# Summing two expert results onto the scaled row with identity matmuls instead of on VectorE and ScalarE

## The chip, the cores and the metric

The kernel runs on 1 core of one Trainium2 chip. The metric is the device time of one execution in microseconds (us). A lower number is better.

## The reference, cut to what matters

A first block ends in a mixture of experts. Each token takes the best two of the 8 experts of its best group, so every token has exactly two results, each with its own weight. The experts' sum is added to ALPHA times the row (ALPHA is the fourth root of 2), a layer norm follows, and the second block opens with an RMS norm of that row.

```python
def _moe(x, wr_g, br_g, wr_e, br_e, w_gate, w_up, w_down):
    ...
        lv, esel = lax.top_k(le, MOE_TOPK)
        we = jax.nn.softmax(lv, axis=-1) * ptop
        ...
        h = jax.nn.silu(hg) * hu * gate[..., None].astype(xs.dtype)
        return jnp.einsum('seh,ehd->sd', h, w_down)

def _layer_norm(x, g, b):
    mu = jnp.mean(xf, -1, keepdims=True)
    var = jnp.mean(jnp.square(xf - mu), -1, keepdims=True)
    return ((xf - mu) * lax.rsqrt(var + LN_EPS) * g + b).astype(x.dtype)

def _rms_norm(x, g, eps=1e-6):
    return (xf * lax.rsqrt(jnp.mean(xf * xf, -1, keepdims=True) + eps) * g).astype(x.dtype)
```

There are 512 tokens of 1024 values, 32 experts with 256 hidden units, and all data is float32.

## The kernel before, in words

The program is a row of **stages** (`Core.stage`, L152). Each stage is one block with a program per engine, and a barrier over all engines closes it, so nothing of a stage starts before the slowest engine of the stage before has come to its end. Inside a stage the engines meet by semaphores only. Three stages matter here.

**choose** (L745 to L870) picks the experts from the router's logits. VectorE carries a long chain; TensorE counts and then builds, for each expert, the list of at most CAP = 64 tokens (L785, one-hot `where` times `whom`). ScalarE takes three exponentials. GpSimd issues two gathers of rows (L804). At the end VectorE writes the two weights of each token into `pair` (L868, L869), token by token.

**experts_by_token** (L989 to L1192) runs the 32 experts one after the other. SyncE (SP) fetches 3 MB of weights for each, into three slots. ScalarE and VectorE split gate and up weights into a rounded part and its rest (L1135, L1176), TensorE multiplies (L1087, L1088), sums (L1096), and forms the results, `down` (L1108). `y_rows` (L1137 to L1143) copies the results of an expert from PSUM by two ScalarE copies of 64x512, and GpSimd scatters them by an indirect DMA (L1054) to `y_dram`, a DRAM buffer with the first results of all tokens in rows 0 to 511 and the second ones in rows 512 to 1023. After the last scatter GpSimd waits until all scatters have landed (L1066, L1067), and then the stage can end. A second way through the program (`results_to_pairs`, L1195), taken when an expert has more than 64 tokens, isn't run with these inputs.

**pairs_end** (L1217 to L1332) takes four tiles of 128 tokens through the following steps, tile by tile:
- SP loads first and second results (L1240, 512 KB each) and, between them, the three rows of gains, each broadcast to 128 partitions (L1242, 512 KB each); then three weight slabs of 1 MB for the next stage (L1244). Two loads of 2 KB that belong to the next stage (`sinks`, L174) stand ahead of all of these.
- ScalarE scales the first result by its weight (`weigh`, L1266). VectorE adds the second result times its weight (L1302) and then ALPHA times the row (L1303).
- ScalarE takes the negative mean (L1275), the sum of squares around it (L1277) and the root (L1278).
- VectorE centres and multiplies by the gain (L1310), inverts the root (L1312), scales and adds the bias (L1315). SP stores that row (L1247).
- ScalarE squares it again and takes a root (L1284, L1285), VectorE inverts (L1326) and makes `h` (L1331), TensorE transposes `h` in eight 128x128 pieces (L1256), ScalarE copies them out rounded (`x_hi`, L1290, two halves) and VectorE takes the rest (`x_lo`, L1321, two halves).

The order on each engine is written out by hand: in round s, VectorE does the sum of tile s, the two row steps of tile s-1, `x_lo` of tile s-2, and `h` of tile s-1. The next stage opens with a weight split (L1477, L1507) and the first matmuls on the rows just made (L1556).

Of the kernel before, what the change touches and what calls it, by code (L numbers as in the profile page):

```python
# [15 lines left out]
F32 = mybir.dt.float32  # L16
# [6 lines left out]
P = 128  # L23
# [721 lines left out]
def choose(c, lg, pair_gates, e, taken, table, most, x_dram, first):  # L745
# [5 lines left out]
    with ExitStack() as ctx:  # L751
# [5 lines left out]
        place, whom = c.sb(ctx, "place", [P, 2, NT]), c.sb(ctx, "whom", [P, 2, NT, 2, NE])  # L757
        where, most_u = c.sb(ctx, "where", [P, 2, NT, CAP]), c.sb(ctx, "most_u", [P, 1], mybir.dt.uint32)
        ps = c.ps(ctx, "lists", [P, 2, 512])
        to_exp, exps, chain, picked, counted, listed, placed, most_ready, cleared, stored = (  # L760
            c.sem(x) for x in ("to_exp", "exps", "dve", "picked", "counted", "listed", "placed", "most_ready", "cleared", "stored"))
        counts = ps[:, 0, 0:(NT + 1) * NE].rearrange("p (i e) -> p i e", e=NE)
        ahead, total = counts[:, 0:NT, :], counts[:, NT, :]
        lists = ps[0:CAP, 1, 0:2 * NE].rearrange("p (w e) -> p w e", w=2)
        xg, gi, xg_in, indexed = first
        with c.stage() as block:
# [7 lines left out]
            def _(pe):  # L774
# [34 lines left out]
            def _(dve):  # L809
# [58 lines left out]
                run(nc.vector.tensor_copy(pair_gates[:, :, 0:1], st[:, :, 4:5]))  # L868
                run(nc.vector.tensor_tensor(pair_gates[:, :, 1:2], st[:, :, 1:2], st[:, :, 4:5], ALU.mult))  # L869
# [119 lines left out]
def experts_by_token(c, table, x_dram, y_dram, w_gate, w_up, w_down, room_yg, small, wgu, wd, gu_in, d_in, first):  # L989
# [8 lines left out]
    with ExitStack() as ctx:  # L998
# [11 lines left out]
        scattered = [c.pool_dma_sem("scattered") for _ in range(2)]  # L1010
# [7 lines left out]
        with c.stage() as block:  # L1018
# [13 lines left out]
            def _(pool):  # L1032
# [33 lines left out]
                for u in range(2):  # L1066
                    pool.wait_ge(scattered[u], 16 * NE // 2)  # L1067
# [55 lines left out]
            def _(act):  # L1123
# [13 lines left out]
                def y_rows(j):  # L1137
# [57 lines left out]
def results_to_pairs(c, y, y_dram, pair):  # L1195

    nc = c.nc
    with ExitStack() as ctx:
        none = c.sb(ctx, "none", [P, D])
        filled, stored = c.sem("filled"), c.sem("stored")  # L1200
        with c.stage() as block:
            @block.sync
            def _(sp):
                sp.wait_ge(filled, 3)
# [3 lines left out]
                sp.wait_ge(stored, 16 * (NT + 1))  # L1208

            @block.vector  # L1210
            def _(dve):
                nc.vector.memset(none[:], 0.0).then_inc(filled, 1)
                nc.vector.memset(pair[:, :, 0:1], 1.0).then_inc(filled, 1)
                nc.vector.memset(pair[:, :, 1:2], 0.0).then_inc(filled, 1)


def pairs_end(c, y_dram, pair, room, rows_to, gain, bias, pre, x_hi, x_lo, opening):  # L1217
# [3 lines left out]
    with ExitStack() as ctx:  # L1221
        r, gb, h = c.sb(ctx, "pairs", [P, 2, NT, D]), c.sb(ctx, "gains", [P, 3, D]), c.sb(ctx, "h", [P, 2, D])
        sq, st, eps = c.sb(ctx, "sq", [P, D]), c.sb(ctx, "stat", [P, NT, 8]), c.sb(ctx, "eps", [P, 2])
        ps = c.ps(ctx, "turned", [P, 8, 512])
        rows_out = c.sem("rows_out")
        gains_in = [c.sem("gains_in") for _ in range(3)]
        pair_in = [c.sem("pair_in") for _ in range(NT)]
        eps_ready, weighed, summed, meaned, rooted, rowed, pre_rooted, h_ready, turned, x_rounded, x_split, chain, act_chain = (
            c.sem(x) for x in ("eps", "weighed", "summed", "meaned", "rooted", "rowed", "pre_rooted", "h", "turned", "x_rounded",
                               "x_split", "dve", "act"))  # L1230

# [3 lines left out]
        with c.stage() as block:  # L1235
            @block.sync
            def _(sp):
                for i in range(NT):
# [2202 lines left out]
```

## Time and profile before

| | |
|---|---|
| median of 3 runs | 2440.09 us (2439.96 to 2444.48) |
| the profiled execution's own time | 2443.96 us |
| its span, first to last instruction | 2442.1 us |
| mean granted TensorE clock | 0.931 of full speed |
| busy share: TensorE, VectorE, ScalarE, GpSimd | 90%, 56%, 37%, 5% |
| choose | from 771.4 to 793.5 us of the span |
| experts_by_token | from 793.5 to about 1104.9 us |
| pairs_end | from about 1110.4 to 1165.0 us |

In the rows, PE is TensorE's matmul, PEld its weight load, DVE is VectorE, ACT ScalarE, POOL GpSimd and SP SyncE. An engine's name with a q (SPq, POOLq) is its instruction queue. PEclk is the clock that TensorE was granted: 1.00 is 2.4 GHz and 0.50 is 1.2 GHz. A number in square brackets is idle time of the engine before the instruction, with what ended it.

### The profile page before, as it was taken

What the parts mean: (1) busy time and instruction counts of PE and PEld (TensorE: products, weight loads), DVE (VectorE), ACT (ScalarE), POOL (GpSimd) and SP (SyncE); (2) the same over time, 40 slices, a digit from 0 to 9 for tenths busy, and PEclk for the clock granted to TensorE, in tenths of its full rate; (3) what the DMA queues carried; (4) which work ended last, traced back from release to release, by engine and by line L of the source; (5) the groups of instructions that cost most, each with busy time, mean ns of one, the idle gap of its engine ahead of it and who ended that gap; (6) DMA issues with size and microseconds to landing.
All of it is one profiled execution on the core that took longest, in us unless ns stands there. A gap on an engine that the chain in (4) does not pass through costs nothing. (4 is left out here: it accounts for less than half of the span.)

```text
span 2442.1 us, 30103 instructions
## 1 busy us (share of the span) xinstructions
PE 2202.9 (90%) x11232; PEld 1664.2 (68%) x11232; DVE 1360.9 (56%) x2391; ACT 906.1 (37%) x1538; POOL 122.2 (5%) x153
## 2 busy tenths in 40 slices
PE   6798998899996999991899989999979998899997
PEld 4587765556776666650777768888757766788886
DVE  2652446856445655544345585964444456778544
ACT  3521233123232666654333433332333334233323
POOL 0000002200000232320000000000000000000000
PEclk8885999999997999995999989999989999999999
DMA  5220431231423899975332113322423222141313
GB/s 162 88 74 1 125 93 54 62 100 44 124 91 143 317 366 358 369 269 184 99 100 66 65 61 104 99 87 87 143 78 103 79 62 65 57 143 64 108 48 112
DMA packets 218989, 296.45 MB, mean 121 GB/s; under 512 B 48861, under 2 KB 183085, under 8 KB 210617
## 3 DMA queue, kind: packets, MB, share of 16 engines
q1 hardware_dynamic: 213722, 286.09, 35.0%
q0 software_dynamic: 5120, 8.40, 1.1%
q8 instruction: 92, 1.51, 0.3%
q14 instruction: 55, 0.45, 0.1%
HBM read 283.12 MB, written 22.07 MB: 125 GB/s over the span
## 5 line engine op out<-in xcount | busy, mean ns | idle before, releaser
L1556 PE MATMUL acc<-x_hi,w_hi 128*128 128x512 f32 x1432 | 579.3, 405 | 19.5 <-DVE w_lo L1507 16.2
L1557 PE MATMUL acc<-x_lo,w_hi 128*128 128x512 f32 x1432 | 566.0, 395 | 0.0
L1558 PE MATMUL acc<-x_hi,w_lo 128*128 128x512 f32 x1432 | 565.2, 395 | 0.0
L1477 ACT CAST w_hi<-raw 128x1024 fp32r<-128x1024 f32 x179 | 186.9, 1045 | 621.5 <-PE acc L1558 587.0
L1507 DVE TENSOR_TENSOR w_lo<-raw,w_hi 128x1024 fp32r<-128x1024 f32 x174 | 212.7, 1224 | 292.6 <-ACT w_hi L1477 289.3
L1556 PEld LDWEIGHTS acc<-x_hi,w_hi 128*128 128x128 f32 x1432 | 273.8, 191 | 84.2 <-DVE w_lo L1507 17.2
L1558 PEld LDWEIGHTS acc<-x_hi,w_lo 128*128 128x128 f32 x1432 | 273.2, 191 | 60.3
L1557 PEld LDWEIGHTS acc<-x_lo,w_hi 128*128 128x128 f32 x1432 | 274.0, 191 | 57.9 <-issue 2.0
L1176 DVE TENSOR_TENSOR w_lo<-wgu,w_hi 128x1024 fp32r<-128x1024 f32 x128 | 151.0, 1220 | 61.3 <-ACT w_hi L1135 60.7
L1135 ACT CAST w_hi<-wgu 128x1024 fp32r<-128x1024 f32 x128 | 127.9, 1047 | 38.6 <-DMA wgu<-in_moe_w_up 33.2
L1108 PE MATMUL ps<-wd,y 128*64 128x512 f32 x256 | 116.7, 598 | 0.7 <-DVE y L1192 0.7
L1087 PE MATMUL ps<-w_hi,xs 128*128 128x512 f32 x256 | 104.2, 407 | 3.3 <-DVE w_lo L1176 3.0
L1088 PE MATMUL ps<-w_lo,xs 128*128 128x512 f32 x256 | 101.4, 396 | 0.0
L1694 ACT ACTIVATE probs<-scores,stat 128x256 f32<-128x256 f32 (+3 forms) x96 | 51.8, 540 | 126.1 <-DVE stat L1656 125.9
L1516 DVE SCALAR_TENSOR_TENSOR sg<-sg,br 128x512 f32<-128x512 f32 x112 | 76.3, 682 | 35.4 <-PE br L1745 28.2
L2291 DVE SCALAR_TENSOR_TENSOR y_t<-pad,w,y_t 128x512 f32<-128x512 f32 x120 | 90.1, 751 | 3.4
L1703 ACT COPY probs_t<-t_ps 128x256 f32<-128x256 f32 (+3 forms) x96 | 39.0, 406 | 130.5 <-PE t_ps L1617 130.5
L1743 PE MATMUL br<-y_hi,b_hi 128*128 128x512 f32 x176 | 70.9, 403 | 15.6 <-DVE b_lo L1735 15.3
L1488 ACT ACTIVATE sg<-acc 128x512 f32<-128x512 f32 x112 | 66.2, 591 | 30.3 <-PE acc L1558 30.2
L1556 PE MATMUL acc<-x_hi,lead_hi 128*128 128x512 f32 x184 | 76.0, 413 | 1.3 <-PEq L157 1.0
L1557 PE MATMUL acc<-x_lo,lead_hi 128*128 128x512 f32 x184 | 73.5, 399 | 0.0
L1558 PE MATMUL acc<-x_hi,lead_lo 128*128 128x512 f32 x184 | 73.4, 399 | 0.0
(554 smaller groups left out, 3357.7 us busy)
## 6 DMA issues: line engine op xcount, KB each, us to landing
raw<-in_w_in SPq DMA_DIRECT2D x60, 1024.0 KB, 5.5
raw<-in_w_gate SPq DMA_DIRECT2D x40, 1024.0 KB, 5.5
wgu<-in_moe_w_gate SPq DMA_DIRECT2D x32, 1024.0 KB
wgu<-in_moe_w_up SPq DMA_DIRECT2D x32, 1024.0 KB
wd<-in_moe_w_down SPq DMA_DIRECT2D x32, 1024.0 KB, 5.3
raw_b<-in_w_branch SPq DMA_DIRECT2D x56, 256.0 KB, 2.8
room<-in_w_out SPq DMA_DIRECT2D x3, 2048.0 KB, 8.4
y_t<-in_w_out SPq DMA_DIRECT2D x3, 2048.0 KB, 10.8
```

The source lines that it names most:

```text
L1087: pe.matmul(ps[:, 0, :], xs[:, u, k, :], w_hi[:, k, :], start=(k == 0), stop=False)
L1088: mm = pe.matmul(ps[:, 0, :], xs[:, u, k, :], w_lo[:, k, :], start=False, stop=(k == KT - 1))
L1108: mm = pe.matmul(ps[0:CAP, 1 + 2 * u + half, :], ht[:, u, m * CAP:(m + 1) * CAP], wd[:, j % SLOTS, m, half * 512:half * 512 + 512], start= ...
L1135: nc.scalar.copy(part(w_hi, p), raw_part(j, p)).then_inc(w_rounded, 1)
L1176: nc.vector.tensor_tensor(part(w_lo, p), raw_part(j, p), part(w_hi, p).bitcast(F32), ALU.subtract).then_inc(w_split, 1)
L1477: self.nc.scalar.copy(self.w_hi[n % 2], self.weights(n)).then_inc(self.rounded, 1)
L1507: eng.tensor_tensor(self.w_lo[n % 2], self.weights(n), self.w_hi[n % 2].bitcast(F32), ALU.subtract).then_inc(self.split, 1)
L1516: self.nc.vector.scalar_tensor_tensor(sg, sg, 1.0, self.br[:], ALU.add, ALU.mult).then_inc(self.mixed, 1)
L1556: pe.matmul(acc, hi, tile.hi[:, k, :], start=(k == 0), stop=False)
L1557: pe.matmul(acc, hi, tile.lo[:, k, :], start=False, stop=False)
L1558: mm = pe.matmul(acc, lo, tile.hi[:, k, :], start=False, stop=(k == KT - 1))
L2291: run(nc.vector.scalar_tensor_tensor(conf[:, m, :], src, wt, conf[:, m, :], ALU.mult, ALU.add))
```

## The change

- **choose** makes no weights by token. It spreads each token's two weights over the experts (`share`, two VectorE multiplications of 128x128) and collects them by expert and place in the list with eight more matmuls (`where` times `share`, 32 columns each) and one ScalarE copy of 64x32 into `weights`.
- **y_rows** multiplies each result row by its weight as it is copied out: the two copies become two activations of the kind Copy with a scale for each partition.
- **experts_by_token** no longer waits for the scatters at its end; SP waits for them in pairs_end, ahead of its loads of results.
- **pairs_end** has TensorE sum: ALPHA times the identity times the row (2 matmuls of 128x128 by 128x512 float32 for each tile), and the identity times the first and the second result (2 matmuls each), all into the same two PSUM banks. `weigh`, L1302 and L1303 go. ScalarE and VectorE read the sum from PSUM. VectorE now does the row steps of tile s in round s, then `h` of tile s-1, then `x_lo` of tile s-2.
- The first row of gains is loaded ahead of all others, the small `sinks` loads come last.

```diff
@@ choose @@
+                pe.wait_ge(shared, 2)
+                for r in range(2):
+                    for i in range(NT):
+                        mm = pe.matmul(of_lists, where[:, r, i, :], share[:, r, i, :], start=(r == 0 and i == 0), stop=(r == 1 and i == NT - 1))
+                mm.then_inc(weighed, 1)
...
+                act.wait_ge(weighed, 1)
+                nc.scalar.copy(weights, of_lists)
...
-                run(nc.vector.tensor_copy(pair_gates[:, :, 0:1], st[:, :, 4:5]))
-                run(nc.vector.tensor_tensor(pair_gates[:, :, 1:2], st[:, :, 1:2], st[:, :, 4:5], ALU.mult))
+                run(nc.vector.tensor_tensor(st[:, :, 5:6], st[:, :, 1:2], st[:, :, 4:5], ALU.mult))
+                for r in range(2):
+                    nc.vector.tensor_tensor(share[:, r], sel[:, r], st[:, :, 4 + r:5 + r].broadcast_to([P, NT, NE]), ALU.mult
+                                            ).then_inc(shared, 1)
@@ experts_by_token @@
-                for u in range(2):
-                    pool.wait_ge(scattered[u], 16 * NE // 2)
...
-                        nc.scalar.copy(yg[:, u, half * 512:half * 512 + 512], ps[0:CAP, 1 + 2 * u + half, :]).then_inc(y_out, 1)
+                        nc.scalar.activation(yg[:, u, half * 512:half * 512 + 512], ps[0:CAP, 1 + 2 * u + half, :], ACT.Copy,
+                                             scale=weights[:, j:j + 1]).then_inc(y_out, 1)
@@ pairs_end @@
+                sp.dma_start(gb[:, 0, :], gain.partition_broadcast(P)).then_inc(gains_in[0], 16)
+                for u in range(2):
+                    sp.wait_ge(scattered[u], 16 * NE // 2)
                 for i in range(NT):
                     for n in range(2):
-                        sp.dma_start(r[:, n, i, :], y_dram[n * S + i * P:n * S + (i + 1) * P, :]).then_inc(pair_in[i], 16)
-                    if i:
-                        sp.dma_start(gb[:, i - 1, :], (gain, bias, pre)[i - 1].partition_broadcast(P)).then_inc(gains_in[i - 1], 16)
+                        sp.dma_start(r[:, n, i, :], y_dram[n * S + i * P:n * S + (i + 1) * P, :]).then_inc(pair_in[i][n], 16)
+                    if i < 2:
+                        sp.dma_start(gb[:, i + 1, :], (bias, pre)[i].partition_broadcast(P)).then_inc(gains_in[i + 1], 16)
                 for dst, src, loaded in opening:
                     sp.dma_start(dst, src).then_inc(loaded, 16)
+                for dst, src in late:
+                    sp.dma_start(dst, src).then_inc(late_in, 16)
...
+                def rows(i):
+                    for half in range(2):
+                        pe.matmul(ps[:, 2 * i + half, :], by_alpha[:], room[:, i, half * 512:half * 512 + 512], start=True, stop=False)
+
+                def results(i):
+                    for n in range(2):
+                        pe.wait_ge(pair_in[i][n], 16)
+                        for half in range(2):
+                            mm = pe.matmul(ps[:, 2 * i + half, :], c.const("ident"), r[:, n, i, half * 512:half * 512 + 512],
+                                           start=False, stop=(n == 1))
+                    mm.then_inc(summed, 1)
...
+                pe.wait_ge(consts_ready, 3)
+                rows(0)
+                rows(1)
+                for i in range(NT):
+                    results(i)
+                    if i + 2 < NT:
+                        rows(i + 2)
+                    if i >= 2:
+                        turn(i - 2)
+                turn(NT - 2)
+                turn(NT - 1)
...
-                def weigh(i):
-                    act.wait_ge(pair_in[i], 32)
-                    nc.scalar.activation(r[:, 0, i, :], r[:, 0, i, :], ACT.Copy, scale=pair[:, i, 0:1]).then_inc(weighed, 1)
...
-                        z = r[:, 0, s, :]
-                        run(nc.scalar.activation(sq[:], z, ACT.Copy, scale=-1.0 / D, accum_out=st[:, s, 0:1]))
+                        run(nc.scalar.activation(sq[:], sums(s), ACT.Copy, scale=-1.0 / D, accum_out=st[:, s, 0:1]))
...
-                        dve.wait_ge(weighed, s + 1)
-                        run(nc.vector.scalar_tensor_tensor(z, r[:, 1, s, :], pair[:, s, 1:2], z, ALU.mult, ALU.add))
-                        nc.vector.scalar_tensor_tensor(z, room[:, s, :], ALPHA, z, ALU.mult, ALU.add).then_inc(summed, 1)
...
+                        dve.wait_ge(rooted, s + 1)
+                        run(nc.vector.scalar_tensor_tensor(x, sums(s), st[:, s, 0:1], gb[:, 0, :], ALU.add, ALU.mult))
+                        run(nc.vector.reciprocal(st[:, s, 3:4], st[:, s, 2:3]))
...
+                        nc.vector.scalar_tensor_tensor(x, x, st[:, s, 3:4], gb[:, 1, :], ALU.mult, ALU.add).then_inc(rowed, 1)
```

`turn(i)` is the loop of transposes that stood there before (L1253 to L1258), `sums(i)` is the pair of PSUM banks of tile i, and `by_alpha` is ALPHA times the identity, made on VectorE when the stage opens.

## Rows read from the trace of the kernel before

**Rows 1.** Busy time by stretch (us; busy us and count; PEclk, DMA share, GB/s).

```profile
1097.00:1101.50 4.50, 3.65 (x8) 1.01 (x8) 0.05 (x1) 1.16 (x2) 0.93 (x2) 1.00 0.17 37
1101.50:1103.50 2.00, 0.00 (x0) 0.00 (x0) 0.00 (x0) 0.00 (x0) 0.90 (x1) 1.00 0.03 8
1103.50:1111.00 7.50, 0.00 (x0) 0.00 (x0) 0.00 (x0) 0.00 (x0) 0.00 (x0) 0.50 0.08 18
1167.50:1171.50 4.00, 4.00 (x9) 3.15 (x10) 1.08 (x1) 0.00 (x0) 0.00 (x0) 0.50 0.74 207
1172.00:1174.00 2.00, 2.00 (x11) 1.60 (x10) 0.00 (x0) 0.00 (x0) 0.00 (x0) 1.00 0.65 231
```

**Rows 2.** Timeline at the edges of pairs_end (start us, us, instruction).

```profile
1102.21 0.90 POOL L1054 DMA_INDIRECT y_scratch<-y_t,si  x1 [4.28 <-ACT y_t L1143]
1110.94 0.81 SPq L174 DMA_DIRECT2D sinks<-in_attn_sink  x2
1118.16 1.15 ACT L1266 ACTIVATE pairs<-pairs,pair 128x1024 f32<-128x1024 f32 x1 [16.79 <-DMA pairs<-y_scratch]
1120.66 1.15 ACT L1266 ACTIVATE pairs<-pairs,pair 128x1024 f32<-128x1024 f32 x1 [1.36 <-DMA pairs<-y_scratch]
1163.55 1.29 DVE L1321 TENSOR_TENSOR x_lo<-turned,x_hi 128x512 fp32r<-128x512 f32 x2 [2.68 <-ACT x_hi L1290]
```

**Rows 3.** GpSimd's queue at the end of experts (first) and of choose (durations ns).

```profile
L157 POOLq DRAIN  x1: 5132/5132/5132, 1105.1 to 1105.1; - x1
...
L157 POOLq DRAIN  x1: 4772/4772/4772, 788.6 to 788.6; - x1
```

**Rows 4.** Timeline of VectorE, one round of pairs_end.

```profile
1133.63 1.28 DVE L1302 SCALAR_TENSOR_TENSOR pairs<-pairs,pair 128x1024 f32<-128x1024 f32 x1
1134.95 1.22 DVE L1303 SCALAR_TENSOR_TENSOR pairs<-room,pairs 128x1024 f32<-128x1024 f32 x1
1136.09 1.28 DVE L1310 SCALAR_TENSOR_TENSOR room<-pairs,stat,gains 128x1024 f32<-128x1024 f32 x1
1137.60 1.28 DVE L1315 SCALAR_TENSOR_TENSOR room<-room,stat,gains 128x1024 f32<-128x1024 f32 x1
1140.91 1.29 DVE L1321 TENSOR_TENSOR x_lo<-turned,x_hi 128x512 fp32r<-128x512 f32 x2 [2.03 <-ACT x_hi L1290]
1142.31 1.28 DVE L1331 SCALAR_TENSOR_TENSOR h<-room,stat,gains 128x1024 f32<-128x1024 f32 x1
1143.51 1.28 DVE L1302 SCALAR_TENSOR_TENSOR pairs<-pairs,pair 128x1024 f32<-128x1024 f32 x1
```

**Rows 5.** Timeline of ScalarE and TensorE in pairs_end.

```profile
1124.44 1.28 ACT L1278 ACT_TABLE_LOAD   x1
...
1136.21 1.06 ACT L1275 ACTIVATE sq<-pairs 128x1024 f32<-128x1024 f32 x1 [4.01 <-DVE pairs L1303]
...
1138.75 0.29 ACT L1278 ACTIVATE stat<-stat,eps 128x1 f32<-128x1 f32 x1
1138.95 1.04 ACT L1284 ACTIVATE sq<-room 128x1024 f32<-128x1024 f32 x1
...
1140.32 1.05 ACT L1290 CAST x_hi<-turned 128x512 fp32r<-128x512 f32 x2
...
1160.93 1.97 PE L1256 MATMUL turned<-consts,h 128*128 128x128 f32 x8 [5.44 <-DVE h L1331]
```

**Rows 6.** Timeline of experts, float32 results and their copies for one expert.

```profile
952.36 3.65 PE L1108 MATMUL ps<-wd,y 128*64 128x512 f32 x8
...
956.04 0.58 ACT L1143 COPY y_t<-ps 64x512 f32<-64x512 f32 x1 [1.08 <-PE ps L1108]
...
957.08 0.28 ACT L1163 ACTIVATE y<-ps 128x128 f32<-128x128 f32 x1 [0.46 <-PE ps L1096]
```

**Rows 7.** Timeline of the end of choose.

```profile
784.80 1.97 PE L785 MATMUL lists<-whom,where 128*64 128x64 f32 x16 [2.45 <-DVE where L853]
...
788.30 0.33 DVE L870 TENSOR_TENSOR taken<-mr,st 128x160 f32<-128x160 f32 x1
```

More of the change, by code:

```diff
@@ L742, in dve_end, with choose @@
         run(nc.vector.tensor_tensor(y, y, self.gate, ALU.mult))
-def choose(c, lg, pair_gates, e, taken, table, most, x_dram, first):
+def choose(c, lg, weights, e, taken, table, most, x_dram, first):
     nc, B = c.nc, 40
@@ L986, in _, with experts_by_token @@
                             nc.vector.tensor_tensor(dst, dst, ps[:, 4 + a % 4, :], ALU.add).then_inc(y_free, 1)
[L989 removed]
+def experts_by_token(c, table, weights, scattered, x_dram, y_dram, w_gate, w_up, w_down, room_yg, small, wgu, wd, gu_in, d_in, first):
     nc, U32 = c.nc, mybir.dt.uint32
@@ L1212, in _, with pairs_end @@
                 nc.vector.memset(none[:], 0.0).then_inc(filled, 1)
-                nc.vector.memset(pair[:, :, 0:1], 1.0).then_inc(filled, 1)
-                nc.vector.memset(pair[:, :, 1:2], 0.0).then_inc(filled, 1)
-def pairs_end(c, y_dram, pair, room, rows_to, gain, bias, pre, x_hi, x_lo, opening):
+def pairs_end(c, y_dram, scattered, room, rows_to, gain, bias, pre, x_hi, x_lo, opening, late):
     nc = c.nc
@@ L1316, in _ @@
-                    if 0 <= s - 2 < NT:
-                        i = s - 2
-                        for half in range(2):
-                            k = slice(4 * half, 4 * half + 4)
-                            dve.wait_ge(x_rounded, 2 * i + half + 1)
-                            nc.vector.tensor_tensor(x_lo[:, k, i * P:(i + 1) * P], turned_rows(i, half),
-                                                    x_hi[:, k, i * P:(i + 1) * P].bitcast(F32), ALU.subtract).then_inc(x_split, 1)
+                        x = room[:, s, :]
@@ L1332, in _ @@
                                                        ALU.mult).then_inc(h_ready, 1)
+                    if 0 <= s - 2 < NT:
+                        i = s - 2
+                        for half in range(2):
+                            k = slice(4 * half, 4 * half + 4)
+                            dve.wait_ge(x_rounded, 2 * i + half + 1)
+                            nc.vector.tensor_tensor(x_lo[:, k, i * P:(i + 1) * P], turned_rows(i, half),
+                                                    x_hi[:, k, i * P:(i + 1) * P].bitcast(F32), ALU.subtract).then_inc(x_split, 1)
 def fill_with(c, pairs):
@@ L2968, in first_block @@
             c.to_fetch.append((wd[:, n], moe[2][n].rearrange("(k p) n -> p k n", p=P), d_in[n]))
-        choose(c, lg[:], pair, e[:], taken[:], table, dram["most"], dram["x"], first)
+        choose(c, lg[:], weights[:], e[:], taken[:], table, dram["most"], dram["x"], first)
         most = nc.values_load(dram["most"], min_val=0, max_val=S)
@@ L3313, in _, with second_block @@
                     nc.vector.tensor_tensor(lg[:, i, :], o.ps[:, i, 0:36], wr_bias, ALU.add)
-def second_block(c, a, y_t, room, pair, dram, out):
+def second_block(c, a, y_t, room, scattered, dram, out):
     nc = c.nc
@@ L3343, in second_block @@
             plans.append((window, queries, hgrn, of_window, of_memory, conv, [merge(n) for n in (0, 2, 1)]))
-        c.load_beside([(sinks[:, n], a["attn_sink_2"][n].partition_broadcast(P)) for n in range(2)])
-        pairs_end(c, dram["y"], pair, room, dram["rows"], a["ln_g"][0, 1], a["ln_b"][0, 1], a["norm_pre_2"][0], x_hi, x_lo,
-                  stream.opening())
+        pairs_end(c, dram["y"], scattered, room, dram["rows"], a["ln_g"][0, 1], a["ln_b"][0, 1], a["norm_pre_2"][0], x_hi, x_lo,
+                  stream.opening(), [(sinks[:, n], a["attn_sink_2"][n].partition_broadcast(P)) for n in range(2)])
         for l, (window, queries, hgrn, of_window, of_memory, conv, of_rest) in enumerate(plans):
@@ L3412, in two_blocks @@
         y_t, lbs, room = c.sb(ctx, "y_t", [P, 10, S]), c.sb(ctx, "lbs", [P, 2, 4]), c.sb(ctx, "room", [P, NT, D])
-        pair = c.sb(ctx, "pair", [P, NT, 2])
-        first_block(c, a, y_t, room, lbs, pair, dram)
-        second_block(c, a, y_t, room, pair, dram, out)
+        scattered = [c.pool_dma_sem("scattered") for _ in range(2)]
+        first_block(c, a, y_t, room, lbs, scattered, dram)
+        second_block(c, a, y_t, room, scattered, dram, out)
         c.settle()
```

64 lines of the change are left out of this document (29 added, 35 removed).

## The prediction

> **What bounds the kernel now.** I read the busy time by stretch first, then the timeline at the edges of pairs_end, then GpSimd's queue, then one round of VectorE and of ScalarE. The clock rows show that TensorE is idle for a long time around the change: it runs at full clock until 1101.5, keeps that clock for two more idle microseconds, and is at half clock from 1103.5 to 1111 and again when the next stage starts, until 1171.5 [rows 1]. The edges show where this comes from [rows 2]. The last scatter is issued at 1102.21, the first load of pairs_end at 1110.94, the first tile of results is in at 1118.16, and the last `x_lo` ends at 1163.55 + 1.29 = 1164.8. GpSimd's queue shows what lies between scatter and stage: a drain that starts at 1105.1, right after the wait for the scatters, and takes 5.13 us [rows 3]. So the stage opens at R = 1110.2, and pairs_end lasts 54.6 us from R.
>
> Inside it VectorE sets the pace. One round lasts 1143.51 - 1133.63 = 9.88 us, of which 2.03 us are idle [rows 4]. The two sums of pairs (L1302, L1303) take 1136.09 - 1133.63 = 2.46 us of it. ScalarE and TensorE have room: ScalarE waits 4.01 us for L1303 in this round [rows 5].
>
> **Part 1, the edge.** The wait for the scatters leaves GpSimd, whose queue can go to its drain once the last scatter is handed over, at about 1102.3. In choose, where nothing is waited for either, the drain starts at 788.6 and takes 4.77 us, to 793.4 [rows 3]. If the drain costs about 5 us from its start, it now ends near 1107.4: 2.8 us saved. The bounds: if the 5.13 us count from the end of the scatter's own 0.90 us (1103.1), the end is 1108.2, 2.0 us saved. If only a short clean-up follows the last indirect DMA, the end could be near 1105.8, 4.4 us saved. I take 2.8, since choose is the nearest row without a wait. SP's new wait comes at about R + 1.2, later than 1105.1, so it finds the scatters landed and the loads behind it lose nothing. The last result copy gets a scale operand: a Copy with a scale for each partition takes 1.15 us for 1024 elements (L1266, [rows 2]) where a Copy with a constant takes 1.06 (L1275, [rows 5]), so 0.1 us is added once on the path.
>
> **Part 2, experts.** The other 63 copies get the same 0.1 us. They lie in waits: 1.08 us ahead of the second copy, 0.46 us ahead of the Silu behind it [rows 6]. Cost 0. If that cover were gone it would be 64 x 0.1 = 6.4 us.
>
> **Part 3, choose.** One small copy goes, two multiplications of 128x128 come (bounded by L870's 0.33 us for 128x160 each), then eight matmuls of 32 columns (at most the 1.97 us of L785's eight with 64) and one small copy [rows 7]. VectorE ends near 789, TensorE near 791, ScalarE before 792. The drain holds the stage until 793.4 [rows 3]. Cost 0; without the drain it would be some 3 us.
>
> **Part 4, pairs_end.** Off VectorE go 4 x 2.46 = 9.8 us, off ScalarE four `weigh` of 1.15. TensorE gets 24 float32 matmuls. Four of them took 3.65 us at full clock [rows 6], which is 0.85 each and a short tail; at half clock I take twice that, 1.7. The new limits for each tile: TensorE 6 x 0.85 = 5.1 us; ScalarE 2.74 (1136.21 to 1138.95) + 1.37 (1138.95 to 1140.32) + 1.05 = 5.2 us [rows 5]; VectorE 9.88 - 2.46 - 2.03 = 5.4 us [rows 4]; loads 2.5 us for each MB (1118.16 to 1120.66, [rows 2]), so 3.75 with a row of gains. All are near 5.3 where 9.88 was. The schedule then follows from the written order, in us after R:
> - TensorE starts at 1.2. At half clock for some 4.3 us, as in the next stage, where 1167.5 to 1171.5 still shows 0.50 and 1172 shows 1.00 [rows 1]. The four matmuls with `by_alpha` end at 6.8.
> - Loads: the first MB was in at R + 7.9. The `sinks` issues ahead of it go (-0.8), a row of gains comes (+1.25): tile 0 at 8.3, then 11.9, 15.7, and 18.2 for the last.
> - Sums on TensorE end at 10.6, 15.8 and 20.9, with the next tile's row matmuls between.
> - Behind a sum ScalarE needs 2.74 + 0.29 = 3.0 us to the root, once with a table load of 1.28 [rows 5]; VectorE then 2.8 (L1310 to the end of L1315) [rows 4]. Root 0 at 14.9, row 0 at 17.7. The second norm's root of tile 0 follows root 1 (18.7) at 20.0, and `h` 0 follows row 1 (21.5) at 23.0.
> - Here TensorE stands: its order puts the transposes of tile 0 ahead of the sum of tile 3. Transposes 24.2, sum of tile 3 at 27.6 instead of 24.3. This is the new wait of the change, 3.3 us.
> - Root 3 at 30.6, row 3 at 33.4, `h` 3 behind `x_lo` of tile 1 at 37.5, transposes 1.97 [rows 5] to 39.5, last `x_lo` 1164.84 - (1160.93 + 1.97) = 1.9 later [rows 2, 5], at 41.4.
>
> 54.6 becomes 41.4: 13.2 us saved. VectorE's L1310 reads PSUM now; no row here has its 1024 form from PSUM, so I take the 1.28 of SBUF, with 0.1 more for each of four tiles as the upper bound.
>
> **The sum.** -2.8 + 0.1 + 0 + 0 - 13.2 = -15.9 us. Against the profiled execution (2443.96 us, span 2442.1) that gives 2428.1. This execution is 3.9 us over the median of the runs shown, so the median becomes 2440.1 - 15.9 = 2424.2 us. The stages ahead and behind are closed by barriers and shift whole; the next one starts at half clock now [rows 1] and has nothing to lose.
>
> **Rivals.**
> *The clock falls back between bursts.* TensorE now waits twice: from 6.8 to about 8, for the first results, and from 20.9 to 23.0, for `h` 0. Against it: TensorE kept 1.00 for 2 us after its last matmul [rows 1]. For it: both gaps are near that length. Each fall puts up to 4.3 us of matmuls at half clock, 2.1 us lost each time: 2424.2 + 4.2 = 2428.4. Chance 0.1.
> The Trainium skill, TensorE: Matmul & The Clock Gate, HAM oscillation, states the rule behind this: bursts of matmuls with DMA waits between them can start cold each time. It speaks against this change; by it the sum is 2428.4 instead of 2424.2, and the 2 us kept at 1.00 speak for the milder answer.
> *The clock never rises in pairs_end.* Before, it stayed at 0.50 through all the transposes. Then a tile's six matmuls take 10.2 us and TensorE is the bound: sums end at 14.9, 25.1, 35.4 and, behind the transposes, 44.2, the stage at 58.1. That is 3.5 us longer than before, less the edge: 2440.9 us, no gain. Against it: solid matmuls raised the clock after 4 us in the next stage [rows 1]. Chance 0.05.
> *A table load with each weighted copy (slower).* The copies in `y_rows` become activations between Silus. If Copy were not in Silu's table, there would be two loads of 1.28 us for each expert, and it decides as soon as they exceed the 0.46 us ahead of the Silu [rows 6], which the TensorE result of the next expert waits for: 32 x (2.56 - 0.46) = 67 us, so about 2491. Against it: L1266 is such a Copy and ran at 1118.16, with a Silu the last function before, and its engine's 16.79 us of idle time ended with the load of results [rows 2]; the load row of the stage stands later, at L1278 [rows 5]. Chance 0.02.
> *The drain takes what the wait gives.* If the drain ends when it did, at 1110.2, whatever starts it, part 1 is worth nothing: 2427. Chance 0.08.
>
> **How the numbers follow.** The forecast has 0.75; its own spread is 2.0 to 4.4 for the edge and some 2 us either way for the loads and the TensorE order, so 2421 to 2427. The range 2419.5 to 2431 adds the burst case and the drain case and leaves out the cold and the table case. A measurement of this kernel can tell about 0.2% (4.9 us) from no change. Faster by more than that, below 2435.2: 0.92. Within: 0.05, the cold clock. Slower: 0.03, the table loads and what I don't see.
>
> **What would show it.** The profile after should have: GpSimd's drain starting near 1102 and SP's first load near 1108; L1302 and L1303 gone and a VectorE round of some 5.5 us; PEclk 1.00 from about 6 us into the stage; a gap of TensorE of about 2 us ahead of the first transposes; a stage of about 41 us; no ScalarE table load in experts after its first Silu; experts as long as before, from 793.5 on. The forecast is wrong if PEclk stays 0.50 in pairs_end, if the second half of the stage waits for TensorE for another reason than `h`, or if experts lengthens by 6 us.

## The result and the profile after

The changed kernel takes 2427.07 us (median of 4 runs, 2421.73 to 2430.56) against 2442.28 us (2439.96 to 2444.66) of the kernel before on the same chip. The ratio is 0.993, with an interval from 0.9915 to 0.9945. It is faster, by 13 to 21 us.

The profiled execution of after is its fastest run, 2421.73 us, with a span of 2419.9 us. That span is 22.2 us shorter than the one of before, which is more than the change gives. So the two traces are compared from landmark to landmark.

GpSimd's queue comes first, since the edge hangs on it: the drain at the end of experts, then the one of choose (durations in ns, then when it starts). The rows of after answer to [rows 3].

```profile
L157 POOLq DRAIN  x2: 53/3160/6268, 1096.5 to 1105.3; - x2
...
L157 POOLq DRAIN  x1: 4753/4753/4753, 783.3 to 783.3; - x1
```

The long drain of experts starts at 1096.5 now, at the issue of the last scatter (whose own record starts at 1096.77) instead of behind its landing, and takes 6.27 us (the short one of 53 ns belongs to the next stage). The drain of choose is as before.

The timeline of after from the last scatter to the last `x_lo`, cut to the lines that pace it (start us, us, instruction). It answers to [rows 2, 4, 5].

```profile
1096.77 0.90 POOL L1065 DMA_INDIRECT y_scratch<-y_t,si  x1 [4.27 <-ACT y_t L1152]
...
1103.54 0.33 SPq L1251 DMA_DIRECT2D gains<-in_ln_g  x1
...
1103.97 5.90 PE L1273 MATMUL rows<-room,by_alpha 128*128 128x512 f32 x8 [8.76 <-DVE eps L1331]
...
1113.40 1.02 ACT L1310 ACTIVATE sq<-rows 128x1024 f32<-128x1024 f32 x1 [17.47 <-PE rows L1279]
...
1121.29 1.28 DVE L1338 SCALAR_TENSOR_TENSOR room<-rows,stat,gains 128x1024 f32<-128x1024 f32 x1 [0.94 <-ACT stat L1313]
...
1125.54 1.09 PE L1287 MATMUL rows<-consts,h 128*128 128x128 f32 x8 [1.94 <-DVE h L1351]
...
1126.43 1.28 DVE L1338 SCALAR_TENSOR_TENSOR room<-rows,stat,gains 128x1024 f32<-128x1024 f32 x1 [0.95 <-ACT stat L1313]
...
1126.47 3.60 PE L1279 MATMUL rows<-pairs,consts 128*128 128x512 f32 x8
...
1132.90 1.28 DVE L1338 SCALAR_TENSOR_TENSOR room<-rows,stat,gains 128x1024 f32<-128x1024 f32 x1 [1.07 <-ACT stat L1313]
...
1139.74 1.97 PE L1287 MATMUL rows<-consts,h 128*128 128x128 f32 x8 [0.62 <-DVE h L1351]
...
1142.37 1.29 DVE L1358 TENSOR_TENSOR x_lo<-rows,x_hi 128x512 fp32r<-128x512 f32 x2 [1.30 <-ACT x_hi L1323]
```

From the start of the last scatter to SP's first issue it is 1103.54 - 1096.77 = 6.8 us, where it was 1110.94 - 1102.21 = 8.7 us: 2.0 us saved at the edge. The stage opens with the barrier's event on SP, first of before and then of after:

```profile
L157 SPq EVENT_SEMAPHORE  x1: 17/17/17, 1110.4 to 1110.4; - x1
```

```profile
L157 SPq EVENT_SEMAPHORE  x1: 17/17/17, 1103.0 to 1103.0; - x1
```

So pairs_end lasts 1142.37 + 1.29 - 1103.0 = 40.7 us, where it was 54.4 us: 13.8 us saved. I call these two measures the **edge** and the **stage**, and use them for every run below. Together they are 15.7 us (1.96 + 13.78).

VectorE's round is shorter, 1126.43 - 1121.29 = 5.1 us, and the next one 1132.90 - 1126.43 = 6.5 us. TensorE waits 1.94 us for `h` of tile 0 at 1125.54 and only then does the sum of tile 3.

Busy time by stretch shows TensorE's clock in the new stage (columns as in [rows 1]).

```profile
1103.50:1107.50 4.00, 3.53 (x4) 1.51 (x5) 0.24 (x3) 0.00 (x0) 0.00 (x0) 0.50 0.58 193
...
1109.00:1124.00 15.00, 14.60 (x35) 6.11 (x33) 5.38 (x6) 8.21 (x15) 0.00 (x0) 1.00 1.04 399
1124.00:1131.00 7.00, 4.84 (x19) 2.58 (x20) 5.91 (x9) 5.44 (x11) 0.00 (x0) 1.00 1.09 370
1131.00:1137.00 6.00, 0.78 (x8) 0.54 (x5) 4.82 (x7) 5.24 (x13) 0.00 (x0) 0.89 0.33 132
1137.00:1143.00 6.00, 3.93 (x16) 3.13 (x16) 4.57 (x9) 2.36 (x5) 0.00 (x0) 0.50 0.14 56
```

The stage opens at half clock, has the full clock while the sums run, keeps it through the waits of TensorE up to 1131, and is back at half clock for the last two rounds of transposes, behind TensorE's idle time of 5.4 us up to 1137.15.

### The profile page after: what moved, and what is told of

Same layout as the page of the kernel before. It is cut to its first block and busy times, and to the rows that moved or that the text cites. A ratio compares the mean times of both kernels' runs of the same rounds, so it can differ in the third digit from the quotient of the medians.

```text
span 2419.9 us, 30222 instructions
## 1 busy us (share of the span) xinstructions
PE 2224.6 (92%) x11296; PEld 1673.9 (69%) x11296; DVE 1351.2 (56%) x2385; ACT 908.6 (38%) x1535; POOL 121.1 (5%) x153
## 5 line engine op out<-in xcount | busy, mean ns | idle before, releaser
L1770 PE MATMUL br<-y_hi,b_hi 128*128 128x512 f32 x176 | 70.9, 403 | 15.7 <-DVE b_lo L1762 15.5
```

## The experiments

**Two theories of the 13.8 us.** Theory A is that of the prediction: the stage is shorter because sums and weights leave VectorE and ScalarE. Theory B: it is shorter because VectorE's order is another one. Before, round s did sum s, row s-1, `x_lo` s-2, `h` s-1. After, it does row s, `h` s-1, `x_lo` s-2, so a tile passes one round less and `h` no longer stands behind `x_lo`.

**VectorE's order alone.** The kernel before, with nothing changed but the order of VectorE's instructions in pairs_end. The sums of tile s + 1 open round s, the row steps are those of tile s, and the loop of `x_lo` moves as it stands behind `h`. The first row step waits for the root now, as in the changed kernel.

```diff
+                def add(i):
+                    z = r[:, 0, i, :]
+                    dve.wait_ge(weighed, i + 1)
+                    run(nc.vector.scalar_tensor_tensor(z, r[:, 1, i, :], pair[:, i, 1:2], z, ALU.mult, ALU.add))
+                    nc.vector.scalar_tensor_tensor(z, room[:, i, :], ALPHA, z, ALU.mult, ALU.add).then_inc(summed, 1)
+
+                add(0)
                 for s in range(NT + 2):
+                    if s + 1 < NT:
+                        add(s + 1)
...
-                        x = room[:, i, :]
-                        dve.wait_ge(meaned, s)
...
+                        x = room[:, s, :]
+                        dve.wait_ge(rooted, s + 1)
...
```

> The kernel before with one thing of the change: VectorE's order. The sum of tile s+1 stands ahead of the row steps of tile s, the row steps of tile s are done in round s, then h of tile s-1, then x_lo of tile s-2. Weights, scatter wait, loads and TensorE are as before. The measure is the time from the stage's opening barrier to the end of the last x_lo: 54.6 us before, 40.7 after. Theory A (what the prediction charged: the gain of the stage is VectorE's 4 x 2.46 us moved to TensorE, and the order only a little): about 50 to 52 us, 3 to 4 saved. Theory B (the old order made VectorE wait for ScalarE and ScalarE for VectorE, so the order is the larger part): a round is then the 7.9 us of VectorE's work without idle time, which gives 44 us and about 10 saved, so a median near 2432.

The time is 2429.51 us (median of 6 runs), ratio 0.9949 (0.9929 to 0.9969). The edge is as before (8.72 us) and the stage takes 44.4 us. Busy time of the whole stage, of before and then of this kernel:

```profile
1110.40:1164.84 54.44, 7.87 (x32) 6.28 (x32) 31.16 (x38) 25.68 (x45) 0.00 (x0) 0.50 0.55 203
```

```profile
1105.30:1149.70 44.40, 7.87 (x32) 6.27 (x32) 31.00 (x38) 25.76 (x45) 0.00 (x0) 0.50 0.67 250
```

The same 38 instructions of VectorE take the same 31 us. What went is idle time of VectorE, 23.3 us down to 13.4. TensorE is at half clock throughout in both. So 10.0 of the 13.8 us come without any work moved to TensorE. Theory B holds for the larger part.

**VectorE sums in the changed kernel.** The changed kernel, weights applied as the results are copied out, but the sums made by VectorE and none by TensorE.

```diff
         def sums(i):
-            return ps[:, 2 * i:2 * i + 2, :].rearrange("p b n -> p (b n)")
+            return r[:, 0, i, :]
...
+                def add(i):
+                    for n in range(2):
+                        dve.wait_ge(pair_in[i][n], 16)
+                    run(nc.vector.tensor_tensor(r[:, 0, i, :], r[:, 1, i, :], r[:, 0, i, :], ALU.add))
+                    nc.vector.scalar_tensor_tensor(r[:, 0, i, :], room[:, i, :], ALPHA, r[:, 0, i, :], ALU.mult, ALU.add
+                                                   ).then_inc(summed, 1)
...
```

> The changed kernel with the sums back on VectorE: two additions for each tile (2.46 us), TensorE only transposes, weights still applied as results are copied out. Theory A: the four sums are 9.8 us of VectorE's work in a stage that VectorE limits, so the stage takes 40.7 + 8 to 10 = about 49 to 50 us and the run is 8 to 10 us slower than the changed kernel. Theory B: TensorE's order (transposes of tile 0 ahead of the sum of tile 3) and its 3.4 us for each sum cost nearly as much as they relieve VectorE of: the stage takes 42 to 44 us.

The time is 2431.34 us (median of 7 runs), ratio 0.9951 (0.9936 to 0.9967). Its busy time over the stage, and below it the same of after:

```profile
1103.80:1146.00 42.20, 7.84 (x32) 6.27 (x32) 30.93 (x39) 21.66 (x41) 0.00 (x0) 0.50 0.72 263
```

```profile
1103.00:1143.66 40.66, 29.18 (x80) 14.58 (x80) 21.58 (x31) 21.25 (x41) 0.00 (x0) 0.84 0.73 273
```

The edge is 6.76 us, as in after; the stage takes 42.2 us. Against the order alone (44.4 us) the weights off ScalarE and the new order of loads give 2.2 us; these two were not parted. Against after (40.7 us) the TensorE sums give 1.5 us. They take 9.35 us of work off VectorE for that. The stage's 13.8 us are 10.0 + 2.2 + 1.5, within rounding. The split holds for this order of steps: TensorE sums under VectorE's old order were not run, and there they might have given more.

The traces carry this split. The three medians of the whole kernel can't rank the two experiments: their intervals overlap, and the last section tells why a run moves by some us on its own.

**`x_lo` ahead of `h`.** The changed kernel, with the loop of `x_lo` (tile s - 2) put back ahead of `h` (tile s - 1).

```diff
+                    if 0 <= s - 2 < NT:
+                        i = s - 2
+                        for half in range(2):
...
                     if 0 <= s - 1 < NT:
...
-                    if 0 <= s - 2 < NT:
-                        i = s - 2
-                        for half in range(2):
...
```

> The changed kernel with x_lo of tile s-2 ahead of h of tile s-1 on VectorE, as in the kernel before. Measure: the stage, 40.7 us in the changed kernel. Theory B: VectorE then stands for ScalarE's x_hi while h could run, and h of the last tile comes later: 44 to 46 us. Theory A (order nearly free): 41 to 42 us.

One run gave 2433.27 us. The stage takes 44.6 us, 4.0 more than in after. The timeline of VectorE, last two `x_lo`:

```profile
1145.68 1.29 DVE L1348 TENSOR_TENSOR x_lo<-rows,x_hi 128x512 fp32r<-128x512 f32 x2 [2.68 <-ACT x_hi L1323]
...
1151.04 1.29 DVE L1348 TENSOR_TENSOR x_lo<-rows,x_hi 128x512 fp32r<-128x512 f32 x2 [2.68 <-ACT x_hi L1323]
```

VectorE stands 2.68 us ahead of each, and they are 5.4 us apart: the next `h` isn't begun before the `x_lo` ahead of it is done, so transposes, rounding and `x_lo` of one tile stand beside nothing. It is the 2.68 that stood in the kernel before too [rows 2]. In after the last two are 2.6 us apart. So the place of `h` alone is worth 4.0 us in the changed kernel; what the earlier row steps add was not run by itself.

**The wait of GpSimd put back.** The changed kernel, with the wait for the scatters at the end of experts again.

```diff
                         scatter(j - 1, count)
+                for u in range(2):
+                    pool.wait_ge(scattered[u], 16 * NE // 2)
```

> The changed kernel with the wait for all scatters put back at the end of GpSimd's program in the expert stage. The measure is from the start of the last scatter to SP's first issue in the next stage: 8.73 us before, 6.77 after. If the edge's 2 us are the wait's and the drain counts from the end of GpSimd's work: 8.7 us again, drain 5.1 us. If the drain has a fixed end whatever precedes it: 6.8 us.

One run gave 2433.51 us. The edge is 8.72 us, 2.0 more than in after; the drain starts at 1104.4 and takes 5.13 us as in the kernel before. So the edge of 2.0 us is that wait. But the stage is longer too, 43.1 us, which none of the parts touched would do. The timeline and the stretches of this run show why:

```profile
1110.68 6.67 PE L1275 MATMUL rows<-room,by_alpha 128*128 128x512 f32 x8 [10.71 <-DVE eps L1333]
...
1133.02 1.31 PE L1289 MATMUL rows<-consts,h 128*128 128x128 f32 x8 [1.94 <-DVE h L1353]
...
1134.13 5.11 PE L1281 MATMUL rows<-pairs,consts 128*128 128x512 f32 x8
```

```profile
1132.00:1134.00 2.00, 0.98 (x8) 0.98 (x9) 1.05 (x2) 1.85 (x6) 0.00 (x0) 0.94 1.10 349
1134.00:1136.00 2.00, 2.00 (x5) 0.97 (x4) 1.93 (x3) 1.97 (x5) 0.00 (x0) 0.50 1.12 360
1136.00:1138.00 2.00, 2.00 (x5) 0.89 (x4) 1.97 (x3) 0.21 (x1) 0.00 (x0) 0.71 1.04 415
```

TensorE waited 1.94 us for `h` of tile 0, as long as in after, but here the clock fell behind that wait: the sum of tile 3 behind the transposes took 5.11 us, not 3.60. The clock also rose later at the start of the stage (6.67 us for the first row matmuls, not 5.90). The forecast's rival "the clock falls back between bursts" came true in this run. It had a price of 2.1 us for each fall; here the fall and the late rise together cost 43.1 - 40.7 = 2.4 us. In after and in six other profiles in which TensorE waits 1.94 us at this place the sum behind it took 3.60 us.

**The transposes behind all sums.** Removes TensorE's new wait.

```diff
                     if i + 2 < NT:
                         rows(i + 2)
-                    if i >= 2:
-                        turn(i - 2)
-                turn(NT - 2)
-                turn(NT - 1)
+                for i in range(NT):
+                    turn(i)
```

> The changed kernel with all transposes on TensorE behind all sums, so that the sum of tile 3 doesn't stand behind the transposes of tile 0. In the changed kernel the sum of tile 3 begins after a wait for h of tile 0. If that wait is on the path: sum of tile 3 about 3 us earlier, the stage 1 to 2 us shorter (39 to 40 us against 40.7). If VectorE and ScalarE limit anyway: the stage stays at 40.7.

One run gave 2426.6 us. The stage takes 39.6 us: the order on TensorE costs 1.1 us.

```profile
1125.07 7.03 PE L1279 MATMUL rows<-pairs,consts 128*128 128x512 f32 x16
```

TensorE has no gap between the sums of tiles 2 and 3, where after shows the 1.94 us and 1.09 us of transposes. Of the 3 us by which sum 3 comes earlier, 1.1 reach the end, since the last rounds hang on VectorE as well.

**Matmuls that fill TensorE's idle time.** Six matmuls that nobody reads, called idle below, ahead of the transposes of tile 2, into a bank that is free by then.

```diff
+                def warm(n):
+                    pe.wait_ge(x_split, 2)
+                    for _ in range(n):
+                        pe.matmul(ps[:, 0, :], c.const("ident"), r[:, 0, 0, 0:512], start=True, stop=True)
...
+                warm(6)
                 turn(NT - 2)
...
```

> The changed kernel with six extra float32 matmuls (identity times a tile that is no longer needed, into a free PSUM bank, never read) between the transposes of tiles 1 and 2, where TensorE is idle for 5.4 us and its clock falls to 0.50. If the low clock costs what the rows say (1.97 us against 1.09 for eight transposes): both last transposes take 1.09 us, the last one is on the path, so the stage is 0.9 us shorter, 1.8 if both are. If the clock at the end costs nothing: 40.7 us.

One run gave 2421.5 us. The stage takes 39.75 us, 0.9 less than in after. The timeline shows the six idle matmuls (two records each) and the last two rounds of transposes at full clock, 1.09 and 1.06 us where after has 1.97 twice:

```profile
1131.78 5.42 PE L1297 MATMUL rows<-pairs,consts 128*128 128x512 f32 x12
1137.06 1.09 PE L1287 MATMUL rows<-consts,h 128*128 128x128 f32 x8
...
1139.74 1.06 PE L1287 MATMUL rows<-consts,h 128*128 128x128 f32 x8 [1.59 <-DVE h L1358]
```

So the half clock at the end of the stage costs 0.9 us, what one round of transposes loses by it (1.97 - 1.09): the earlier round lies beside VectorE's work.

**A drain ahead of the last scatters.** GpSimd drains once more where it waits for results anyway.

```diff
                         scatter(j - 1, count)
+                    if j == NE - 2:
+                        pool.drain()
```

> The changed kernel with an extra drain on GpSimd three experts before the end, where its queue is idle for some 7 us. Measure: from the end of the last indirect DMA instruction to the end of the drain: 5.3 us in the changed kernel, 2.7 us at the end of choose, where only two indirect DMAs came before. Theory 1: the drain's length grows with the indirect DMAs since the last one: about 2.7 to 3 us now, the whole run 2.5 us shorter. Theory 2: its length has another cause: 5.3 us as before, and the extra drain costs nothing.

One run gave 2419.42 us. The rows of GpSimd's queue and of the last scatter:

```profile
L1078 POOLq DRAIN  x1: 6130/6130/6130, 1083.6 to 1083.6; - x1
...
L157 POOLq DRAIN  x2: 53/1506/2958, 1097.3 to 1102.8; - x2
```

```profile
1097.54 0.90 POOL L1065 DMA_INDIRECT y_scratch<-y_t,si  x1 [4.27 <-ACT y_t L1154]
...
1101.00 0.33 SPq L1253 DMA_DIRECT2D gains<-in_ln_g  x1
```

The added drain takes 6.13 us at 1083.6, in idle time of GpSimd, and the last one only 2.96. The edge is 3.5 us instead of 6.8, and the stage takes the same 40.7 us. So the drain's length isn't fixed: the earlier one took more than half of it away.

**The same in the middle of experts.** If the length depends on what was issued since the last drain, half of it should come back.

```diff
-                    if j == NE - 2:
+                    if j == NE // 2:
                         pool.drain()
```

> The changed kernel with an extra drain on GpSimd at the middle of the experts instead of three before the end, so that 29 indirect DMAs lie between it and the last drain (2 with the drain three before the end, 62 without). The last drain ended 1.9 us after the last indirect DMA instruction with 2, 5.3 us with 62. If the length grows evenly with their number: 1.9 + 27/60 x 3.4 = 3.4 us. If it grows up to some number only, as a queue that fills: near 5.3 us.

```profile
L1078 POOLq DRAIN  x1: 8002/8002/8002, 958.2 to 958.2; - x1
...
L157 POOLq DRAIN  x1: 4056/4056/4056, 1109.6 to 1109.6; - x1
```

Counted from the end of the last scatter's own 0.90 us, the drain ends 1096.5 + 6.27 - 1097.67 = 5.1 us later in after, with 30 gathers and 32 scatters since the drain before. It is 1.8 us with the early drain (2 scatters) and 2.9 us here (13 gathers and 16 scatters), where an even growth was to give 3.4. These three grow with the number of indirect DMAs.

The number alone doesn't give the length, though. The two added drains, counted the same way from the scatter ahead of them, end 1083.6 + 6.13 - 1084.79 = 4.9 us behind it with 60 indirect DMAs since the drain of choose, and 958.2 + 8.00 - 959.34 = 6.9 us behind it with only 33. The stretches of these two, the early one first, differ in what the DMA engines did beside them:

```profile
1084.80:1089.70 4.90, 4.90 (x17) 2.50 (x16) 0.00 (x0) 1.27 (x2) 0.00 (x0) 1.00 0.14 29
```

```profile
959.30:966.20 6.90, 6.90 (x28) 3.60 (x26) 5.23 (x5) 5.55 (x7) 0.04 (x1) 1.00 1.03 431
```

The DMA share was 0.14 in the first and 1.03 in the second. Whether that makes the longer one was not tested. The drain in the middle isn't free either: it took 8.0 us there, held a gather up, and experts lasted 291.7 us from first to last scatter instead of 284.9. One run gave 2434.73 us. The place of an added drain decides more than the drain.

**Plain copies in experts.** Leaves the weights of the results out.

```diff
-                        nc.scalar.activation(yg[:, u, half * 512:half * 512 + 512], ps[0:CAP, 1 + 2 * u + half, :], ACT.Copy,
-                                             scale=weights[:, j:j + 1]).then_inc(y_out, 1)
+                        nc.scalar.copy(yg[:, u, half * 512:half * 512 + 512], ps[0:CAP, 1 + 2 * u + half, :]).then_inc(y_out, 1)
```

> The changed kernel with the results copied out plainly, without their weights, so the weights are left out of the result. Measure: the 31 experts between the first and the last scatter, about 290 us, and mean ns of a copy, 579 against about 680. If the 0.1 us of each of 64 copies is hidden in waits: the same length within 0.3 us. If it is on the path: 6 us shorter than in the changed kernel.

The line of the copies in this kernel, and then in after (ns: least, mean, most):

```profile
L1152 ACT COPY y_t<-ps x64: 580/580/587, 812.9 to 1099.6; 64x512 f32<-64x512 f32 x64
```

```profile
L1152 ACT ACTIVATE y_t<-ps,weights x64: 682/682/690, 808.6 to 1095.2; 64x512 f32<-64x512 f32 x64
```

A scale for each partition costs 102 ns for each copy, and nothing in the end: from first to last scatter both take 284.9 us, and the kernel before 285.1. Experts has one table load of 1.28 us, ahead of its first Silu, in this kernel, in after and in before; none stands behind it. One run gave 2427.32 us.

**Three mends together.** The early drain, the transposes behind all sums, and idle matmuls ahead of the transposes of tiles 1 and 2, in the changed kernel.

```diff
...
+                turn(0)
+                pe.wait_ge(rowed, 2)
+                warm(2, 2)
+                turn(1)
+                pe.wait_ge(x_split, 2)
+                warm(0, 4)
+                turn(2)
+                turn(3)
```

> The changed kernel with three things together: the early drain (three experts before the end), transposes behind all sums, and extra float32 matmuls in TensorE's waits (two ahead of the transposes of tile 1, four ahead of those of tile 2) so that its clock stays at 1.00. If the three add up: from the last scatter to SP's first issue 3.5 us (6.8 in the changed kernel), stage 40.7 - 1.1 - 0.9 = 38.7 us, and the run 5 us faster than the changed kernel, about 0.991 of the kernel before. If the late transposes and the kept clock save the same time, the stage is 39.6 us.

The time is 2420.16 us (median of 4 runs, 2419.84 to 2420.58), ratio 0.9908 (0.9893 to 0.9923) against the kernel before. The changed kernel, run again beside it:

> The changed kernel again, as it is, to set its time beside the others on one chip and to have a second profile of it. If its stage is steady: from the last scatter to SP's first issue 6.8 us and 40.7 us of stage, whatever the rest of the run does. If its clock in the stage varies as it did in the run with the wait put back: up to 43 us.

It takes 2428.63 us (median of 5 runs, 2426.8 to 2431.68), ratio 0.9942 (0.9928 to 0.9956), edge 6.77 and stage 40.66 us. So the trace of after is reproduced to 0.1 us in both measures. The three mends bring 8.5 us by the medians and 3.3 + 2.0 = 5.3 us by the traces: the edge is 3.46 us and the stage 38.65. The parts add up (1.1 and 0.9 make the 2.0). The profiled executions of the two differ by 8.2 us in span (2426.2 and 2418.0): 1.7 us lie ahead of the last scatter and 1.2 behind the stage, in code that is the same in both. What makes these I can't tell. Stretches of this kernel:

```profile
1126.00:1134.00 8.00, 6.84 (x28) 3.69 (x27) 6.94 (x9) 7.50 (x17) 0.00 (x0) 1.00 1.03 364
1134.00:1143.00 9.00, 5.11 (x23) 2.66 (x21) 8.21 (x13) 4.92 (x11) 0.00 (x0) 1.00 0.16 63
```

**Idle matmuls up to the next stage.** Two more behind the last transposes, so that the next stage might open at full clock.

```diff
                 turn(3)
+                warm(0, 2)
```

> As the three together, with two more extra matmuls behind the last transposes, so that TensorE stands idle about 3 us instead of 4.6 before the next stage's first matmul. In the changed kernel the first 2.7 us of matmuls of the next stage run at 0.50. If the clock is kept over that gap: 1.00 from the first matmul, 1.3 to 1.5 us saved there. If the gap is still too long: 0.50 as before, nothing saved.

One run gave 2419.12 us, with a stage of 38.97 us. The next stage still opened at half clock, behind a wait of 2.63 us:

```profile
1136.00:1140.00 4.00, 3.91 (x12) 2.44 (x12) 2.52 (x5) 1.07 (x2) 0.00 (x0) 0.57 0.00 0
1143.20:1146.20 3.00, 2.99 (x7) 2.41 (x8) 1.09 (x1) 0.00 (x0) 0.00 (x0) 0.52 0.57 162
```

The clock had already gone down in the last round of transposes, which the kernel without the two matmuls passed at 1.00. That fall I can't explain, so whether a clock held up to the barrier would help stays open. As it is the addition brings nothing.

## Why the prediction was right, and where its reasons failed

**The total.** Forecast -15.9 us; by the traces -15.7. The medians differ by 15.2, and the median of 2427.07 us lies 2.9 above the forecast 2424.2; 2.2 of that is the median before, which was taken as 2440.1 and came out at 2442.28. The range and the direction hold. That the total came so close is in part luck: the edge was put 0.8 us too high and the stage 0.6 too low, and the stage's time came out of the schedule while the reason given for it was wrong (part 4).

**Part 1, the edge: mis-sized.** The term was -2.8 and measured -2.0. The failing step is "the drain costs about 5 us from its start", taken from choose. It starts at 1096.5 and takes 6.27 us, so what counts is its end, 5.1 us behind the end of GpSimd's last work. Before, the drain started 2.0 us after that work, at 1105.1, and took 5.13 us: it paid the same length behind the wait. That was the lower bound of the text. In choose the same count gives 788.05 - 785.31 = 2.7 us behind the second of its two gathers, so it was no model for a stage with 62 indirect DMAs. Two scatters gave 1.8 us, so the number is not all there either. What was right: the wait was worth what it lasted, and moving it to SP cost nothing. The rival in which the drain takes all of it falls with the run that put the wait back, 2.0 us slower at the edge.

**Parts 2 and 3: right.** The weighted copy takes 682 ns where it was 0.58 us [rows 6], 0.1 more as forecast, and experts is as long as before. In choose the new matmuls take 1.92 us and the copy stands at 785.28, ahead of the drain's end at 788.05:

```profile
783.33 1.92 PE L794 MATMUL lists<-share,where 128*64 128x32 f32 x16 [1.86 <-DVE share L880]
785.28 0.18 ACT L805 COPY weights<-lists 64x32 f32<-64x32 f32 x1 [3.45 <-PE lists L794]
```

**Part 4, pairs_end: the time right, the cause not.** Its schedule was close. ScalarE reads sum 0 at 1113.40, 10.4 us after the stage opens (10.6 forecast), sum 3 at 27.1 (27.6); TensorE's wait is 1.94 us (2.1); the last transposes end at 38.7 (39.5), the stage at 40.7 (41.4). VectorE's read of PSUM takes the 1.28 us that the text took from SBUF. One wait of the schedule didn't come: TensorE was to stand until about 8 us for the first results, but sum 0 starts at 1109.70, 6.7 us after the stage opens and right behind the row matmuls.

The step that failed is the sentence "Off VectorE go 4 x 2.46 = 9.8 us", with the limits for each tile behind it. It set the two rounds, 9.88 and 5.3 us, against each other as if the sums made the difference. But the schedule was laid out in the new written order, and that order alone takes 10.0 us out of the stage with all 31 us of VectorE's work in it. The weights and the loads take 2.2 us, the TensorE sums 1.5. The forecast read the idle 2.03 us of the round [rows 4] and took them out of the new round (9.88 - 2.46 - 2.03 = 5.4) without a reason; it didn't ask what a tile waits for between its steps. VectorE was busy for 31.2 of 54.4 us of the stage, so its work was no bound, as "VectorE sets the pace" had it: what a tile waits for in the written order was.

**The new wait of TensorE** came where the text put it, in its size. What it costs at the end is 1.1 us, since the sum behind it is not the only thing that the last rounds wait for.

**The clock rivals.** The clock rose in the stage (1.00 from 1109), so the cold case falls. The case of a clock that falls between bursts is open. Of its two waits only the one for `h` came. Of the eight profiles that have this wait of 1.94 us, only the one with GpSimd's wait put back lost the clock behind it, and how often runs without a profile do is not to be seen. Behind the wait of 5.4 us, ahead of the transposes of tile 2, after is at half clock too. The rule cited in the prediction from the Trainium skill, TensorE: Matmul & The Clock Gate, HAM oscillation, is that bursts of matmuls with DMA waits between them start cold. The waits here are for VectorE; the trace agrees behind the 5.4 us, and behind the 1.94 us in one run of eight. The table loads fall: none shows in experts behind the one of the first Silu.

## What to carry to other kernels

Where an engine that seems to set the pace has idle time in its round, lay out the same work in another order before moving any of it: here the order gave 10.0 us, and 9.4 us of work taken off VectorE gave 1.5. The wait that stood ahead of GpSimd's end of a stage cost its own length, 2.0 us. The drain behind it costs more after many indirect DMAs than after few; one more drain, early and in idle time, took 3.3 us off the path, and one in the middle of the stage made that stage 6.8 us longer. Compare traces of two kernels from landmark to landmark, since an unchanged stage can shift them by as much as the change does.

## What the runs showed of the hardware that was not expected

**The drain's length.** The end of GpSimd's part of experts came 1.8, 2.9 and 5.1 us behind the last scatter's own work, with 2, 29 and 62 indirect DMAs since the drain before. But it was 2.7 us behind two gathers in choose, 4.9 late in experts after 60, and 6.9 in the middle of experts after only 33, where the DMA share was 1.03. So something besides the number sets it, and that stays open. What it does in that time no trace shows.

**The same code at two clocks.** Code far ahead of the change differs between profiles. Stretches of before, then of after:

```profile
120.00:125.00 5.00, 5.00 (x61) 5.00 (x60) 3.62 (x6) 0.68 (x2) 0.00 (x0) 0.55 0.22 56
125.00:130.00 5.00, 5.00 (x53) 5.00 (x52) 2.05 (x3) 0.00 (x0) 0.00 (x0) 0.50 0.02 3
```

```profile
120.00:125.00 5.00, 5.00 (x90) 4.93 (x89) 4.59 (x8) 0.00 (x0) 0.00 (x0) 1.00 0.10 34
125.00:130.00 5.00, 5.00 (x64) 4.80 (x62) 1.49 (x3) 4.54 (x9) 0.00 (x0) 1.00 0.44 70
```

The records in these stretches are not all of the same lines, since after is further on. One run of 128 small matmuls can be compared, in before and then in after:

```profile
118.83 11.46 PE L577 MATMUL ps<-ar,bkbe 64*64 64x64 f32 x128 [1.79 <-DVEq L440]
```

```profile
117.43 7.14 PE L577 MATMUL ps<-ar,bkbe 64*64 64x64 f32 x128 [1.18 <-DVEq L440]
```

It is 4.3 us longer where the clock fell. The first gather of choose starts at 788.27 in before and at 782.95 in after, 5.3 us earlier, and nothing in between was changed. Of the fourteen profiles, eight were granted 0.50 in the second stretch (before, the repeated changed kernel and the three mends together among them) and six 1.00 (after, the order alone and VectorE sums among them). Between after and its repetition the spans differ by 6.3 us, with the same edge and stage. This goes a long way to explain why the changed kernel spreads from 2421.7 to 2431.7 us, but runs without a profile don't show their clock there, so for the medians it is argued, not shown.

**The clock behind equal waits.** After a wait of 1.94 us, with nearly the same work ahead of it, TensorE kept full clock in after and lost it in the run with the wait put back. What tells the two apart stays open.
